# Two z slots of a fused two-block network moved ahead of the first round, by token tiles

## The chip, the cores and the metric

One core of one Trainium2 chip runs the whole program in one launch. The metric is the device time of one execution in microseconds (us), read as the median of the runs.

## The reference, cut to what matters

256 tokens of width 1024 pass through a first block of two layers and then a second block. The change lies at the start of the second block's mixer:

```python
h = rms_norm_2(x, g_mix[i])
proj = h @ w_in[i]
glu_a, glu_b, q, k, v, z, a_in, b_in, gate_a, gate_b = split_cols(proj, IN_SIZES)
...
qkv = silu(depthwise_conv(concat([q, k, v]), qkv_conv_w[i]))
g = -exp(a_log[i]) * softplus(a_in + dt_bias[i])      # a_in: 16 columns
beta = sigmoid(b_in)                                  # b_in: 16 columns
o_fwd = gated_delta_rule(q, k, v, g[:, :, 0], beta[:, :, 0])
...
o = rms_norm_2(o_fwd + o_bwd, delta_norm_g[i]) * silu(z)
```

x entering h is itself the output norm of the first block, so two norms follow one another there: the double norm (numbers 4 and 5 in the kernel). a_in and b_in together are the 32 columns called ab; z has 1024 columns.

## The kernel before, in words

**Weights.** All weights come as one stream of slots, in the order of stream_plan. A slot is 128 x 2048 float32 (1 MB): for a "pair", two tiles of 128 output columns over all eight tiles of the inner dimension; the slot of ab holds 32 columns only. SP's queue loads a slot into one of three raw buffers as soon as the slot three before is split. ACT rounds it to whi (split, L1784, or split_half, L1793) when TensorE is done with the slot three before. wlo = raw - whi is made by DVE (L2314), by POOL (L1075, in halves; for most slots of the rounds), or by both, POOL taking the first half (split_shared, L993) and DVE the second (L2310): the SHARED_SLOTS. Before, ab is DVE's, the slot ("qk", 0) is shared, and ("v", 0) is DVE's.

**Products.** The helper three (L1134 to L1136) makes hi x hi, hi x lo and lo x hi. A slot of the rounds takes 2 x 8 x 3 = 48 matrix multiplies, most of them feature-major: weights stationary, 256 tokens moving. A z slot is token-major: 128 tokens of the normalized input stationary, 256 weight columns moving; m of half_slot is then the token tile. ab is token-major too, before: 48 multiplies with 32 columns moving (ab_products).

**The double norm.** norm_behind_down(4, ...) on ACT and on DVE follows the down projection of the first block's last layer, whose last three slots are multiplied for token tile 0 first and then for tile 1. For each token tile: DVE adds the sums to x (L2442), multiplies by the gain (gain_x, L2425), scales (scale_x, L2433) and normalizes again (L2346); ACT takes the sums of squares (L1811, L1803); POOL the powers (L971, and L978 to L981). TensorE turns the tile to feature-major (turn_norm, L1158), ACT rounds it (L1866), DVE makes its low half (lows, L2416). Between these steps ACT and DVE split the coming slots, in a fixed order.

**TensorE's order.** turn_norm(5, 0), ab for tile 0, six spins (spin, L1141: a multiply of the identity that fills time, two records each), turn_norm(5, 1), two spins, ab for tile 1, then the rounds. Bank 3 of PSUM holds ab's sums.

**The rounds.** There are ten, of eight ticks each. A slot fills two ticks, two parts in each, and between the parts stand small multiplies of one of eight heads: prepare (turns, L1439 at tick 3; L1449 at tick 5; L1466 and L1470 at tick 6), the inverse by levels for the head of the round before (level_turn L1491 at tick 0, steps L1509 to L1531), and the chain of the head before that (L1574 to L1601). DVE works the 31 taps of a long convolution into each tick beside that (L2762, TAP_COUNT in each tick). Rounds 0 to 4 have four slots, rounds 5 to 9 have three but the last. Before, round 1 holds qk1, z0, glu2, glu3, and round 3 qk3, z2, glu5, z3.

**Round 0 around the change.** DVE copies ab from its bank and prepares it (decay_inputs, L2648 to L2654), then splits the slot of ("v", 0); ACT at tick 1 takes exp, ln and tanh (decay_logs, L2185 to L2189, with a table load before each), between two halves of a split; DVE makes the decays at tick 2; ACT evacuates qk0 at tick 2 (L2004), DVE adds its taps (L2699), ACT takes tanh (L2026), DVE gates (L2740), TensorE turns the result at tick 3 (L1439), and at tick 4 sums the decays (L1418 to L1423).

The wait of half_slot on a bank's earlier reader (slot_read) goes by the ordinal of a slot in MIX_SLOTS, two banks taking turns.

## Time and profile before

| | before |
|---|---|
| median of 3 runs | 1242.95 us (1240.95 to 1244.08) |
| span of the profiled execution | 1239.0 us |
| PE (matrix multiplies) busy | 1211.3 us, 98% |
| PE weight loads busy | 1109.0 us, 90% |
| DVE busy | 846.4 us, 68% |
| ACT busy | 703.4 us, 57% |
| POOL busy | 300.7 us, 24% |

The span runs from the first to the last instruction. The profile gives no other time for its own execution; the runs' median is 3.95 us above its span, which is what lies around the span. Positions below are us from the start of the span. Rows are of three kinds: the chain of work that ended last, the timeline (start, duration, engine, line, operation, output<-inputs, shapes, count, and in brackets the idle time before it with what ended it), and windows (busy time and number of instructions of each engine in a stretch, the granted clock of TensorE where 1.00 is full speed, the share of DMA time and GB/s).

### The profile page before, as it was taken

To read this page: it belongs to the slowest core of one execution; us is meant where nothing else is said; L and a number is where in the kernel's file an instruction comes from. 1 tells how busy PE (TensorE), PEld (TensorE's weight loads), DVE (VectorE), ACT (ScalarE), POOL (GpSimd) and SP (SyncE) were. 2 spreads that over 40 slices of the span, in tenths; PEclk is the share of its full clock that TensorE was granted. 3 is DMA by queue.
4 is the path that set the end of the run, shared out by engine and by line. 5 is a ranking of instruction groups with operands and counts; after the bars stand their busy time and mean duration, and the time that the engine had idled before them with its cause. 6 is when DMAs were issued, how large, how long until landed. Compare 5 with 4: busy or idle time off the path is not lost.

```text
span 1239.0 us, 21308 instructions
## 1 busy us (share of the span) xinstructions
PE 1211.3 (98%) x8590; PEld 1109.0 (90%) x8590; DVE 846.4 (68%) x1507; ACT 703.4 (57%) x1181; POOL 300.7 (24%) x251
## 2 busy tenths in 40 slices
PE   9999999999999999999999999999999999999997
PEld 7776899998877799998899999999988989999886
DVE  6796588874675678885558787788853555555457
ACT  5465576663467566664466666767665445444344
POOL 2170100000024000000166667565645210000000
PEclk9999999999999999999989999999998999999999
DMA  7633355555553355555333232232223555555542
GB/s 282 239 140 138 119 210 194 204 186 175 180 190 108 141 210 206 196 183 203 137 136 136 103 137 103 103 137 91 83 85 116 193 187 204 194 178 197 180 159 85
DMA packets 31586, 199.74 MB, mean 161 GB/s; under 512 B 4289, under 2 KB 6481, under 8 KB 8706
## 3 DMA queue, kind: packets, MB, share of 16 engines
q1 hardware_dynamic: 29506, 189.27, 42.3%
q0 software_dynamic: 1840, 8.60, 1.8%
q8 instruction: 68, 1.11, 0.4%
q10 hardware_dynamic: 144, 0.52, 0.1%
q14 instruction: 28, 0.23, 0.1%
HBM read 197.33 MB, written 1.05 MB: 160 GB/s over the span
## 4 chain that ended last, share of the span: by engine, by line
PE 85%; DVE 7%; ACT 4%; issue 2%; POOL 1%; DMA 0%; POOLq 0%; SPq 0%; ACTq 0%; DVEq 0%
PE ps L1134 25%; PE ps L1136 24%; PE ps L1135 24%; PE ps L1509 1%; PE ps L1525 1%; DVE ps L2762 1%; PE ps L1287 1%; PE ps L1306 1%; PE ps L1274 1%; PE ps L1158 1%; DVE conv L2699 1%; PE ps L1141 1%; PE ps L1227 1%; DVE wlo L2314 1%; ACT whi L1784 0%
## 5 line engine op out<-in xcount | busy, mean ns | idle before, releaser
L1134 PE MATMUL ps<-halves,whi 128*128 128x256 f32 x1472 | 415.7, 282 | 0.0
L1136 PE MATMUL ps<-halves,wlo 128*128 128x256 f32 x1472 | 410.2, 279 | 0.0
L1135 PE MATMUL ps<-halves,whi 128*128 128x256 f32 x1472 | 410.1, 279 | 0.0
L2314 DVE TENSOR_TENSOR wlo<-raw,whi 128x2048 fp32r<-128x2048 f32 (+1 forms) x139 | 315.2, 2270 | 126.0 <-ACT whi L1784 122.4
L1784 ACT ACTIVATE whi<-raw 128x2048 fp32r<-128x2048 f32 (+1 forms) x143 | 270.0, 1890 | 110.9 <-PE ps L1136 106.1
L1134 PEld LDWEIGHTS ps<-halves,whi 128*128 128x128 f32 x1472 | 278.2, 189 | 0.3 <-issue 0.2
L1135 PEld LDWEIGHTS ps<-halves,whi 128*128 128x128 f32 x1472 | 278.0, 189 | 0.1
L1136 PEld LDWEIGHTS ps<-halves,wlo 128*128 128x128 f32 x1472 | 277.9, 189 | 0.0
L1075 POOL TENSOR_TENSOR wlo<-raw,whi 128x1024 fp32r<-128x1024 f32 x72 | 173.9, 2425 | 53.5 <-ACT whi L1793 53.1
L1134 PE MATMUL ps<-whi,halves 128*128 128x512 f32 (+4 forms) x440 | 151.8, 345 | 3.8 <-DVE halves L2416 3.6
L971 POOL TENSOR_TENSOR rstd<-sumsq,half_power 128x1 f32<-128x1 f32 x14 | 11.1, 796 | 594.2 <-ACT xn L1811 422.4
L1136 PE MATMUL ps<-whi,halves 128*128 128x512 f32 (+4 forms) x440 | 147.4, 335 | 0.0
L1135 PE MATMUL ps<-wlo,halves 128*128 128x512 f32 (+4 forms) x440 | 147.1, 334 | 0.0
L1134 PE MATMUL ps<-whi,hhi 128*128 128x512 f32 x264 | 102.8, 390 | 0.5 <-DVE hf L2633 0.5
L1135 PE MATMUL ps<-wlo,hhi 128*128 128x512 f32 x264 | 102.7, 389 | 0.0
L1136 PE MATMUL ps<-whi,hlo 128*128 128x512 f32 x264 | 102.7, 389 | 0.0
L1134 PEld LDWEIGHTS ps<-whi,halves 128*128 128x128 f32 x440 | 83.2, 189 | 17.0 <-issue 8.8
L2762 DVE SCALAR_TENSOR_TENSOR ps<-glu_in,par,ps 128x256 f32<-128x256 f32 x224 | 94.8, 486 | 0.0
L1136 PEld LDWEIGHTS ps<-whi,halves 128*128 128x128 f32 x440 | 83.2, 189 | 9.0
L1135 PEld LDWEIGHTS ps<-wlo,halves 128*128 128x128 f32 x440 | 83.3, 189 | 7.5
L1962 ACT ACTIVATE cv<-ps,par 128x256 f32<-128x256 f32 x88 | 44.9, 561 | 76.8 <-PE ps L1136 70.5
L1793 ACT ACTIVATE whi<-raw 128x1024 fp32r<-128x1024 f32 x72 | 76.5, 1064 | 8.1 <-PE ps L1136 8.1
(333 smaller groups left out, 1821.5 us busy)
## 6 DMA issues: line engine op xcount, KB each, us to landing
raw<-in_stream SPq DMA_DIRECT2D x176, 1024.0 KB, 4.8
gain<-in_gains POOLq DMA_DIRECT2D x7, 512.0 KB, 6.1
bias<-in_rel POOLq DMA_DIRECT2D x1, 1536.0 KB, 9.0
raw<-in_stream SPq DMA_DIRECT2D x2, 648.0 KB, 7.3
cst<-in_consts POOLq DMA_DIRECT2D x1, 1280.5 KB, 5.9
raw<-in_stream SPq DMA_DIRECT2D x2, 528.0 KB, 4.1
x<-in_x SPq DMA_DIRECT2D x2, 512.0 KB, 4.4
out<-xn SPq DMA_DIRECT2D x4, 256.0 KB, 2.2
```

The lines of the kernel that those rows point to most:

```text
L1075: pool.tensor_tensor(wlo[:, n % RING, c], raw[:, n % RAW, c], whi[:, n % RING, c].bitcast(F32), ALU.subtract).then_inc(*S["pool_weights_lo ...
L1134: nc.tensor.matmul(out, a_hi, b_hi, start=start, stop=False)
L1135: nc.tensor.matmul(out, a_hi, b_lo, start=False, stop=False)
L1136: return nc.tensor.matmul(out, a_lo, b_hi, start=False, stop=stop)
L1141: nc.tensor.matmul(ps[:, bank, 0:P], ident, ident, start=True, stop=True)
L1158: last = nc.tensor.transpose(ps[:, 4 + 2 * t + half, i * P:(i + 1) * P], xn[:, t, (4 * half + i) * P:(4 * half + i + 1) * P], ident)
L1227: last = nc.tensor.transpose(ps[:, 3, i * P:(i + 1) * P], temp[:, b % 2, t, i * P:(i + 1) * P], ident)
L1784: act.activation(used(whi, n), used(raw, n), ACT.Copy).then_inc(*S["weights_high"].one((n, 1)))
L1793: act.activation(whi[:, n % RING, c], raw[:, n % RAW, c], ACT.Copy).then_inc(*S["weights_high"].one((n, half)))
L1962: act.activation(cv[:, j % 2, m, :], ps[:, up_bank(j), m * TOK:(m + 1) * TOK], ACT.Identity, bias=par_at(f"conv_b{li}", c), scale=par_at(f ...
L2314: dve.tensor_tensor(used(wlo, n), used(raw, n), used(whi, n).bitcast(F32), ALU.subtract)\
L2762: dve.scalar_tensor_tensor(odd_taps[:, :] if k == 29 else sums, src, w, sums, ALU.mult, ALU.add)\
```

## The change

Two of the four z slots, z0 and z1, leave rounds 1 and 2 (and z2 moves up from round 3 to round 2 into z1's place), so that rounds 1 and 3 have three slots where they had four. z0 and z1 stand ahead of ab in the stream and are multiplied as soon as a token tile of the double norm is there: both for tile 0, two spins, both for tile 1. Both are shared slots. ab comes after them and becomes feature-major: its 32 columns stationary, 256 tokens moving, 24 multiplies. DVE copies the 32 x 256 result to SBUF, TensorE turns it back in the first round behind the first part of qk0, and DVE takes it from there. ACT takes the second square of tile 0 ahead of a split. qk0 and v0 are split by DVE alone, each after the evacuation of a z slot by ACT (tanh) and DVE.

```diff
--- before.py
+++ after.py
@@ -85,6 +85,8 @@
         for j in range(FT):
             pair((f"up{layer}", j), ("ffn_w_up", layer), j * P, FF + j * P)
         down(f"down{layer}", ("ffn_w_down", layer), FT)
+    for key, weight, a, b in OPENING:
+        pair(key, (weight, 0), a, b)
     plan.append(("narrow", "ab", ("w_in_2", 0), 6144, 32))
     for round_ in ROUNDS:
         for key, weight, a, b in round_:
@@ -101,6 +103,11 @@
     return plan
 
 
+def z_slots():
+
+    return [(("z", j), "w_in_2", 5120 + 2 * j * P, 5120 + (2 * j + 1) * P) for j in range(KT // 2)]
+
+
 def rounds():
 
 
@@ -109,9 +116,9 @@
 
     glu = [(("glu", j), "w_in_2", j * P, 1024 + j * P) for j in range(KT)]
     gates = [(("gates", j), "w_in_2", 6176 + j * P, 7200 + j * P) for j in range(KT)]
-    z = [(("z", j), "w_in_2", 5120 + 2 * j * P, 5120 + (2 * j + 1) * P) for j in range(KT // 2)]
+    z = z_slots()
     out = [(("conv_out", i), "w_conv_out_2", 2 * i * P, (2 * i + 1) * P) for i in range(KT // 2)]
-    other = [glu[0:2], [z[0]] + glu[2:4], [glu[4], z[1]], [z[2], glu[5], z[3]], [glu[6], gates[0]],
+    other = [glu[0:2], glu[2:4], [glu[4], z[2]], [glu[5], z[3]], [glu[6], gates[0]],
              [glu[7]] + gates[1:2], gates[2:3], gates[3:5]]
     made = []
     for r in range(HEADS):
@@ -137,6 +144,7 @@
 JOINS_SECOND = {1: 1, 2: 2}
 PRODUCT_BANK = (3, 3, 3, 3, 6, 6)
 ROUNDS = rounds()
+OPENING = z_slots()[0:2]
 
 
 EVEN_BLOCKS = [("idx", 1536, 324), ("qb", 1860, 512), ("kb", 2372, 512), ("vb", 2884, 512),
@@ -353,6 +361,8 @@
     "early_turned": "and feature-major in its bank, (layer, j)",
 
     "gained": "x times the gain of norm 4 in xn, (t, half)",
+    "ab_copied": "decay's and beta's inputs, feature-major, copied from bank 3",
+    "ab_turned": "and token-major in bank 3",
     "ab_abs": "absolute value of the decay's input, all of ab read from its bank",
     "act_step": "exp of minus the absolute value; exp(a_log)",
     "ab_ln": "ln(1 + exp)",
@@ -526,12 +536,12 @@
                   ("proj", 3, 1): (2, 0), ("proj", 3, 2): (2, 1), ("proj", 5, 1): (4, 0), ("proj", 5, 2): (4, 1),
                   ("proj", 6, 1): (5, 0), ("proj", 6, 2): (5, 1)},
          "odd": {("proj", b + 1, 1 + t): (b, t) for b in range(4) for t in range(TT)}}
-SPINS = {0: (2, 3, 0), 1: (8, 2, 0), 2: (0, 0, 4), 3: (8, 2, 0), 5: (0, 0, 2), 6: (0, 4, 0), 7: (0, 0, 0)}
+SPINS = {0: (2, 3, 0), 1: (8, 2, 0), 2: (0, 0, 4), 3: (8, 2, 0), 5: (0, 0, 4), 6: (0, 4, 0), 7: (0, 0, 0)}
 SPIN_BANK = {1: 7, 3: 7}
 LEAD = RING
 EARLY = 2
 SPIN_BANK[5] = 2
-AB_SPINS = (6, 2)
+OPENING_SPINS = (2, 2)
 TURN_ORDER = {layer: list(turns.values()) for layer, turns in TURNS.items()}
 INDEX_AT = {("proj", 2, 1): (0, 1), ("proj", 2, 2): (2, 3), ("proj", 2, 3): (4, 5), ("proj", 3, 0): (6, 7)}
 FORGET_ROWS_AT = ("proj", 1, 3)
@@ -543,7 +553,7 @@
 
 
 
-MIX_SLOTS = [("ab", -1, 0)] + [(slot[0], r, 2 * i) for r, slots in enumerate(ROUNDS) for i, slot in enumerate(slots)] \
+MIX_SLOTS = [(slot[0], -1, 2 * i) for i, slot in enumerate(OPENING)] + [(slot[0], r, 2 * i) for r, slots in enumerate(ROUNDS) for i, slot in enumerate(slots)] \
     + [(("delta_out", i), len(ROUNDS), 0) for i in range(KT // 2)]
 ORDINAL = {key: n for n, (key, _, _) in enumerate(MIX_SLOTS)}
 READ_BY_ACT = {"gates"}
@@ -568,7 +578,7 @@
 
 def tanh_order():
 
-    order = []
+    order = [slot[0] for slot in OPENING]
     for r in range(len(ROUNDS)):
         for i in range(TICKS):
             key = finished_slot(r, i)
@@ -914,7 +924,7 @@
 
         POOL_SLOTS = [slot_of[key] + AHEAD for key, r, tick in MIX_SLOTS if 0 <= r < len(ROUNDS)]
 
-        SHARED_SLOTS = [slot_of[key] for key in (("up0", 1), ("up1", 1), ("qk", 0), ("up2", 1))]
+        SHARED_SLOTS = [slot_of[key] for key in (("up0", 1), ("up1", 1), ("z", 0), ("z", 1), ("up2", 1))]
 
         o_junk = ab[:, 3:5, :, :].rearrange("p a t c -> p (a t c)")
 
@@ -1037,7 +1047,8 @@
                 deviation(4, t)
                 deviation_5(t)
                 if t == 0:
-                    split_shared(("qk", 0))
+                    for key, *_ in OPENING:
+                        split_shared(key)
 
             pool.memset(sum_row[:, :].bitcast(F32), 0.0).then_inc(*S["rows_cleared"].one("mixer"))
             pool.memset(glu_in[:, :, :], 0.0).then_inc(*S["glu_cleared"].one())
@@ -1371,7 +1382,7 @@
                 n, o = slot_of[key], ORDINAL[key]
                 if m == 0 and part == 0:
                     wait_low(pe, n)
-                    if o >= 3:
+                    if o >= 2:
                         pe.wait_ge(*slot_read(MIX_SLOTS[o - 2][0]))
                 if key[0] == "z":
                     wh = used(whi, n).rearrange("p (k c) -> p k c", k=KT)
@@ -1393,19 +1404,32 @@
                 if m == 1 and part == 1:
                     last.then_inc(*S["weights_used"].one(n))
 
-            def ab_products(t):
+            def opening(t):
+
+                turn_norm(5, t)
+                for key, *_ in OPENING:
+                    for half in range(2):
+                        if key == OPENING[0][0]:
+                            wait_split(5, t, (half,))
+                        half_slot(key, t, half)
+
+            def ab_products():
 
                 n = slot_of["ab"]
-                if t == 0:
-                    wait_low(pe, n)
+                wait_low(pe, n)
                 wh, wl = used(whi, n), used(wlo, n)
                 for kt in range(KT):
-                    if kt % 4 == 0:
-                        wait_split(5, t, (kt // 4,))
-                    last = three(ps[:, 3, t * 32:(t + 1) * 32], xhi[:, kt, t * P:(t + 1) * P], xlo[:, kt, t * P:(t + 1) * P],
-                                 wh[:, kt, :], wl[:, kt, :], kt == 0, kt == KT - 1)
-                if t:
-                    last.then_inc(*S["weights_used"].one(n))
+                    last = three(ps[0:32, 3, 0:TOK], wh[:, kt, :], wl[:, kt, :], xhi[:, kt, :], xlo[:, kt, :],
+                                 kt == 0, kt == KT - 1)
+                last.then_inc(*S["weights_used"].one(n))
+
+            def turn_ab():
+
+                pe.wait_ge(*S["ab_copied"].at())
+                for t in range(TT):
+                    last = nc.tensor.transpose(ps[:, 3, TOK + t * 32:TOK + (t + 1) * 32], odd_taps[0:32, t * P:(t + 1) * P],
+                                               ident[0:32, 0:32])
+                last.then_inc(*S["ab_turned"].one())
 
             def decay_sums():
 
@@ -1710,11 +1734,10 @@
                 up(li, 2 * li + 1)
                 down(f"down{li}", FT, hhi, hlo, lambda kt: pe.wait_ge(*S["hidden_low"].at((li, kt))))
 
-            for t in range(TT):
-                turn_norm(5, t)
-                ab_products(t)
-                if t == 0:
-                    spin(*AB_SPINS)
+            opening(0)
+            spin(*OPENING_SPINS)
+            opening(1)
+            ab_products()
             for r in range(len(ROUNDS)):
                 for i in range(TICKS):
                     if r == 0 and i == 4:
@@ -1722,6 +1745,8 @@
                     level_first(r - 1, i)
                     if slot_at(r, i):
                         half_slot(slot_at(r, i), i % 2, 0)
+                    if r == 0 and i == 0:
+                        turn_ab()
                     chain_first(r - 2, i)
                     if i == 7:
                         query_products(r)
@@ -1839,9 +1864,9 @@
 
                 split(last)
                 square(k, 0)
-                split(last + 1)
                 if k == 4:
                     square(5, 0)
+                split(last + 1)
                 split(last + 2)
                 round_turned(5 if k == 4 else k, [(0, 0), (0, 1)])
                 square(k, 1)
@@ -2217,6 +2242,9 @@
                 up(li)
                 norm_behind_down(2 * li + 2, slot_of[(f"down{li}", FT // 2 - 1)])
 
+            for j, (key, *_) in enumerate(OPENING):
+                evacuate(key)
+                split(slot_of["ab"] + 1 + j)
             for r in range(len(ROUNDS)):
                 for i in range(TICKS):
                     if r == 0 and i == 1:
@@ -2641,11 +2669,16 @@
                 dve.tensor_tensor(plo[:, :, :], ps[:, up_bank(FT - 2), :].rearrange("p (k c) -> p k c", k=2),
                                   phi[:, :, :].bitcast(F32), ALU.subtract).then_inc(*S["p_low"].one())
 
+            def copy_ab():
+
+                dve.wait_ge(*S["weights_used"].at(slot_of["ab"]))
+                dve.tensor_copy(odd_taps[0:32, :], ps[0:32, 3, 0:TOK]).then_inc(*S["ab_copied"].one())
+
             def decay_inputs():
 
-                dve.wait_ge(*S["weights_used"].at(slot_of["ab"]))
+                dve.wait_ge(*S["ab_turned"].at())
                 dve.wait_ge(params2_loaded, 16)
-                link(dve.tensor_copy(ab[:, 0, :, :], ps[:, 3, 0:64].rearrange("p (t c) -> p t c", t=2)))
+                link(dve.tensor_copy(ab[:, 0, :, :], ps[:, 3, TOK:TOK + 64].rearrange("p (t c) -> p t c", t=2)))
                 dt = row_at["dt_bias_2"].unsqueeze(1).broadcast_to([P, TT, 16])
                 link(dve.tensor_tensor(ab[:, 0, :, 0:16], ab[:, 0, :, 0:16], dt, ALU.add))
                 link(dve.tensor_scalar(ab[:, 1, :, 0:16], ab[:, 0, :, 0:16], -1.0, None, ALU.mult))
@@ -2948,8 +2981,12 @@
                 up(li)
                 norm_behind_down(2 * li + 2, slot_of[(f"down{li}", FT // 2 - 1)])
 
+            for j, (key, *_) in enumerate(OPENING):
+                split(slot_of["ab"])
+                evacuate(key, 0)
+                split(slot_of["ab"] + 1 + j)
+            copy_ab()
             decay_inputs()
-            split(slot_of["ab"] + AHEAD)
             for r in range(len(ROUNDS)):
                 for i in range(TICKS):
                     if r == 0 and i == 2:
```

## Rows read from the trace of the kernel before

**Rows 1.** The page's chain of work that ended last, share of the span by engine.

```profile
PE 85%; DVE 7%; ACT 4%; issue 2%; POOL 1%; DMA 0%; POOLq 0%; SPq 0%; ACTq 0%; DVEq 0%
```

**Rows 2.** Timeline, PE, opening to round 0's first turn.

```profile
615.03 1.03 PE L1158 MATMUL ps<-ident,xn 128*128 128x128 f32 x8
...
617.27 0.25 PE L1134 MATMUL ps<-whi,halves 128*128 128x32 f32 x1 [1.20 <-DVE halves L2416]
...
620.42 2.91 PE L1141 MATMUL ps<-ident 128*128 128x128 f32 x12
...
628.59 0.36 PE L1134 MATMUL ps<-halves,whi 128*128 128x256 f32 x1
...
633.15 0.28 PE L1135 MATMUL ps<-halves,whi 128*128 128x256 f32 x1
...
635.98 0.28 PE L1135 MATMUL ps<-halves,whi 128*128 128x256 f32 x1
...
641.68 0.66 PE L1439 MATMUL ps<-ident,conv 128*128 128x128 f32 x4
```

**Rows 3.** Window in round 0: us, PE, PEld, DVE, ACT, POOL, clock, DMA, GB/s.

```profile
629.60:633.00 3.40, 3.40 (x19) 3.40 (x17) 2.42 (x4) 3.34 (x6) 2.95 (x1) 0.51 0.00 0
```

**Rows 4.** Windows by round (1, 3, 5, 6, 7), from one L1491 to the next.

```profile
660.74:695.06 34.32, 34.17 (x285) 33.58 (x286) 28.82 (x70) 22.61 (x48) 23.97 (x14) 1.00 0.35 124
...
732.29:768.21 35.92, 35.92 (x307) 35.59 (x306) 29.23 (x70) 24.16 (x55) 24.13 (x17) 1.00 0.33 118
...
805.61:837.30 31.69, 31.07 (x260) 30.19 (x258) 26.45 (x64) 21.24 (x52) 20.14 (x15) 1.00 0.37 134
837.30:871.50 34.20, 32.39 (x262) 31.14 (x263) 29.82 (x73) 23.15 (x56) 19.31 (x14) 1.00 0.27 93
871.50:904.10 32.60, 31.33 (x260) 30.25 (x258) 27.45 (x67) 21.54 (x53) 19.26 (x14) 1.00 0.27 98
```

**Rows 5.** Timeline, ACT, double norm and round 0.

```profile
612.57 1.93 ACT L1784 ACTIVATE whi<-raw 128x2048 fp32r<-128x2048 f32 x1 [1.24 <-PE ps L1136]
...
631.22 0.23 ACT L2185 ACTIVATE ab<-ab 128x32 f32<-128x32 f32 x1
...
634.41 0.23 ACT L2189 ACTIVATE ab<-ab 128x32 f32<-128x32 f32 x1
634.55 1.04 ACT L1793 ACTIVATE whi<-raw 128x1024 fp32r<-128x1024 f32 x1
636.07 0.84 ACT L2004 ACTIVATE conv<-ps,par 128x256 f32<-128x256 f32 x2 [0.47 <-PE ps L1136]
```

**Rows 6.** Timeline, DVE, the same stretch.

```profile
617.63 1.29 DVE L2425 TENSOR_TENSOR xn<-x,gain 128x512 f32<-128x512 f32 x2
...
619.95 1.22 DVE L2310 TENSOR_TENSOR wlo<-raw,whi 128x1024 fp32r<-128x1024 f32 x1
...
628.78 0.23 DVE L2648 COPY ab<-ps 128x64 f32<-128x64 f32 x1 [2.39 <-PE ps L1136]
...
629.74 2.29 DVE L2314 TENSOR_TENSOR wlo<-raw,whi 128x2048 fp32r<-128x2048 f32 x1
```

**Rows 7.** Timeline, POOL, the same stretch.

```profile
614.57 2.36 POOL L993 TENSOR_TENSOR wlo<-raw,whi 128x1024 fp32r<-128x1024 f32 x1 [2.16 <-ACT whi L1784]
617.87 0.86 POOL L971 TENSOR_TENSOR rstd<-sumsq,half_power 128x1 f32<-128x1 f32 x1 [0.94 <-ACT junk L1811]
...
630.05 4.22 POOL L1075 TENSOR_TENSOR wlo<-raw,whi 128x1024 fp32r<-128x1024 f32 x1 [6.88 <-ACT whi L1793]
```

**Rows 8.** Timeline, POOL's and then DVE's half of an earlier shared slot.

```profile
135.94 2.40 POOL L993 TENSOR_TENSOR wlo<-raw,whi 128x1024 fp32r<-128x1024 f32 x1 [43.54 <-ACT whi L1784]
...
137.80 1.62 DVE L2310 TENSOR_TENSOR wlo<-raw,whi 128x1024 fp32r<-128x1024 f32 x1
```

**Rows 9.** Timeline, ACT: a table load ahead of a wait.

```profile
358.28 1.28 ACT L1937 ACT_TABLE_LOAD   x1
362.25 0.40 ACT L1937 ACTIVATE prob<-prob,lowest 128x128 f32<-128x128 f32 x1 [2.69 <-DVE lowest L2579]
```

## The prediction

> **What bounds the kernel now.** I read the chain of waits first: 85% of it is TensorE, 7% DVE, 4% ACT [rows 1]. So a change pays by taking time out of TensorE's order, and costs by making TensorE wait. Then the timeline of TensorE around the change [rows 2]: the down projection ends at 615.03, the turn of tile 0 and a wait of 1.20 us lead to ab at 617.27, spins fill from 620.42, round 0 begins at 628.59, and the first turn of round 0 (L1439) comes at 641.68. These 26.65 us are one half of the question. The other half is rounds 1 and 3, which lose a slot each. The windows by round show what a slot is worth there [rows 4]: round 3 with four slots took 35.92 us, round 7, also without a v slot, 32.60 with three, round 5 31.69.
>
> **What is removed.** Multiplies with 256 moving columns follow one another every (635.98 - 633.15)/24 = 0.118 us at full clock [rows 2], so a slot of 48 is 5.65 us. Two slots leave rounds 1 and 3 on balance: at most 11.3 us. But a product also hides DVE, which stays: the taps per tick don't change, since the tick in which the next glu slot is ready moves only earlier and the counts per tick are used up before and after. Only the evacuations of two z slots, about 0.7 us each on DVE (a 512-wide pass of the same kind is half of a 1.29 us pair [rows 6]), leave the rounds. DVE was busy 26.45, 29.82 and 27.45 us in the three-slot rounds 5, 6 and 7, and these lasted 5.2, 4.4 and 5.2 us more than that [rows 4]: DVE and its waits set their length. Round 3 keeps 29.23 - 0.7 = 28.5 us of DVE, plus 4.7 is 33.2: it gives back 2.7. Round 1 keeps 28.1 us, has no chain yet (fewer dependent steps), and TensorE's own 34.3 - 5.65 = 28.7; I put it halfway between 28.7 and 28.1 + 5 = 33.1, at 31: 3.3 back. Together 6.0 us, bounds 4.4 (both at DVE plus 5) and 11.3.
>
> **The opening, step by step.** Nothing moves up to 615.03. The turn of tile 0 and the wait for its low half stay: 617.3.
>
> - *z0's low half.* Today one shared slot, ("qk", 0), is split by POOL at 614.57 in 2.36 us and by DVE at 619.95 in 1.22 [rows 6, 7]. ACT could round that slot at 612.57 [rows 5]. Now ACT rounds z0 about 611.0 to 612.9 (the second square goes first) and z1 to 614.8. POOL can start z0 at 613.0, but DVE normalizes from two SBUF inputs until 613.6 and then wants its own half of z0. That the two engines keep each other out is in the rows: POOL's 2.4 us split took 4.22 beginning 0.3 us after a DVE split of 2.29 [rows 6, 7], and DVE's 1.22 us half took 1.62 when it met the end of POOL's [rows 8]. With DVE first, POOL has z0 from 614.9 to 617.3, and TensorE starts z0 at 617.45, as now within 0.2 us.
> - *z1's low half.* POOL goes on with z1, 617.3 to 619.7. DVE's gain_x for tile 1, at 617.63 today [rows 6], now meets it and waits to 619.7. POOL's power for tile 1, at 617.87 today [rows 7], comes behind z1 too, at 619.7 or later. gain_x takes 1.29, scaling 0.9, then DVE's half of z1 1.22: ready at about 623.2 where the half that stands there today was ready at 621.17. TensorE ends z0 of tile 0 at 617.45 + 2.83 = 620.3 and stands still until 623.3: 3.0 us. What is queued behind this wait is all of TensorE.
> - *The rest.* z1 of tile 0 2.83; two spins 0.45; turn of tile 1 0.9; four spins 0.9, which nearly cover ACT's and DVE's rounding, 0.2 more; z0 and z1 of tile 1 5.65; ab, 24 multiplies. The trace has none with 32 stationary columns and 256 moving; the bounds are 0.118 as the other 256-wide ones and the low clock's 0.21, and nothing gives a gain over 0.118; taken 0.118, 2.83. Round 0 then begins at 623.3 + 13.75 = 637.05.
> - *Clock.* Where the granted clock was 0.51, TensorE started 19 multiplies in 3.40 us where 0.118 would give 29 [rows 3]: a loss of about 1.3 us each such stretch. Today it fell after the wait at 617.27 and the 32-column multiplies. The new wait of 3 us may bring it down while z1 is multiplied; half a stretch taken, 0.7. Bounds none and two stretches, 2.6.
>
> Round 0 at 637.75, that is 9.15 us later than 628.59.
>
> **Round 0 to its first turn.** Call X the end of z1 for tile 1; TensorE has ab done at X+2.8 and the first part of qk0 at X+4.25.
>
> - *The copy of ab.* ACT evacuates z1 and rounds v0 until X+2.7; DVE has qk0 (2.29), z1's evacuation (0.7), then v0 (2.29) [rows 6] until X+5.2, and only then copies ab, 0.45. TensorE turns it at X+5.8 instead of X+4.25: a wait of 1.55, and 0.3 for the two turns. Behind this wait stands the whole of qk0's second part. The bounds of the copy and the turns, which no row shows: 0.2 (the 64-wide copy took 0.23 [rows 6]) to 0.7, and 0.2 to 0.7.
> - *The logs.* DVE prepares ab until X+7.1. ACT has exp to tanh from 631.22 to 634.64, 3.4 us [rows 5]; the load of exp's table ahead of it is hidden in the wait, as the load at 358.28, which ran at once while its ACTIVATE waited 2.69 us more [rows 9]. The same hides the extra load of tanh's table for z0, while ACT waits for z0's products. So ACT is free at X+10.6, then has half a split, 1.04 [rows 5].
> - *qk0.* Its products end at X+10.3; ACT evacuates it at X+11.65 instead of X+10.4. From there to the turn it took 641.68 - 636.07 = 5.6 us [rows 2, 5]: X+17.25. TensorE is there at X+16.05. A wait of 1.2 where today it is 0.2.
> - *Given back.* The low clock in round 0 today, 1.3 [rows 3].
>
> Sum for this part: 1.55 + 0.3 + 1.0 - 1.3 = +1.55 us. Later steps of round 0 have room: DVE has few taps yet, and the late half of glu0 is low at about X+14, while TensorE needs it at X+20.
>
> **The sum.** +9.15 + 1.55 - 6.0 = +4.7 us on the profiled span, 1239.0 to 1243.7; with the 3.95 us between span and median, 1247.6. I give 1247.5.
>
> **A rule weighed.** The Trainium skill, SBUF — State Buffer, "Who interferes with whom", says that a DVE instruction with two SBUF inputs contends with a GpSimd instruction that reads SBUF, and that whichever issues first keeps the shared pair for its whole instruction while the other stands fully blocked. The trace agrees at both places named above, the 4.22 and the 1.62 us. By a rule of shared bandwidth the two halves of z1 would stretch a little and TensorE's wait would be about 1 us, the sum +2; by this rule it speaks against the change.
>
> **The rivals.**
>
> - *Matrix work is all that counts.* Count only TensorE's own time: the opening 18.7 us long instead of 13.56, +5.1; turns +0.3; clock -1.3; the wait at L1439 -0.2; two slots -11.3: -7.4, 1235.5. For it: 85% of the chain. Against it: the three-slot rounds, which TensorE alone would have ended at 35.92 - 5.65 = 30.3 and which took 31.69 and 32.60 [rows 4]. It decides from where the waits (3.0 for z1, 1.55 for the copy, 1.2 for qk0, 5.3 not given back by the rounds, 0.7 clock, some 0.4 small) come to less than 7.4; to be faster by over 0.3% (3.7 us, about what a measurement of this kernel can tell from no change) they must be under 3.7.
> - *No collision at z1.* POOL and DVE fall so that z1 is ready at 621.2, as the half in its place now [rows 6]: 2.1 less wait and no fall of the clock, 0.7: +1.9, 1244.8. For it: DVE's adds and lows read PSUM and leave POOL room until 617.6. Against it: POOL has 4.8 us of splits from 613.0 on, which end at 617.8 at best.
> - *POOL first.* POOL gets z0 at 613.6, DVE's half waits to 616.0, and the add of tile 1 and the lows of tile 0 stand behind it. TensorE starts z0 at 619.4, after 3.5 us of standing, z1 at about 624.4; the clock falls for at least a stretch. 1.1 + 1.3 more, with a second stretch 3.7: +7 to +8.5, 1250 to 1252. For it: POOL asks for z0 before DVE does. Against: the order at 613.6 is a toss.
> - *The change does nothing it says.* z's multiplies by tiles are as many as before and cost the same, so no work is saved but ab's 24 multiplies; that is in the sum already.
>
> **How the numbers follow.** Chances: forecast 45%, no collision 22%, POOL first or more low clock 18%, matrix work 15%. The forecast's own range is 1244.5 to 1250.5 by the bounds of the clock and the rounds. Slower by over 0.3%, above 1246.7: 29 of the forecast's 45, all 18, 1 of the second, 48%. Faster, below 1239.2: 11 of the last 15 and 2 of the second, 13%. Within: 39%. Range 1240 to 1253, which leaves about 10% below and 8% above.
>
> **What would show it.** Right: in the opening, TensorE idle 2 to 4 us between z0 and z1 of tile 0 with DVE's L2310 as the releaser, and L2425 of tile 1 starting after 619; a wait of 1 to 2 us before the turns of ab, with the copy behind v0's split; L1439 near 652 (+10.7); rounds 1 and 3 near 31 and 33 us. Wrong: z1's first multiply before 621.5; rounds 1 and 3 both under 30.5 us, which would make the kernel faster by more than it loses in the opening; or a fall of the clock of more than two stretches.

## The result: slower by 0.58%

The changed kernel took 1248.88 us (median of 19 runs) beside 1241.9 us for the kernel before, a ratio of 1.0058 with a 95% interval of 1.004 to 1.0077: by the ratio 7.2 us slower (5.0 to 9.6). The lowest, the median and the highest of the 19 runs lie 8.5, 7.0 and 9.7 us above those of the kernel before. The profiled execution took 1249.72 us and has a span of 1247.9. The page of the changed kernel, its span, its busy times and its chain by engine:

```profile
span 1247.9 us, 21256 instructions
...
PE 1210.4 (97%) x8564; PEld 1106.0 (89%) x8564; DVE 854.1 (68%) x1510; ACT 702.5 (56%) x1179; POOL 293.6 (24%) x248
...
PE 82%; DVE 9%; ACT 5%; issue 3%; POOL 1%; DMA 0%; POOLq 0%; DVEq 0%; ACTq 0%
```

TensorE has 26 multiplies fewer and is busy 0.9 us less; the chain has moved to DVE and ACT (from 11% to 14%, [rows 1]). Not all of the 8.9 us between the two spans are the change's. The turn of tile 0 stands at 619.64 instead of 615.03 [rows 2], and TensorE's order ahead of it is the same. The last section comes back to that. From that turn to the last L1491, that of round 8 (L1515 in the changed kernel; rounds 1 to 8 have one each, and the rounds shown in [rows 4] run from one to the next), it is 299.49 us instead of 289.05: +10.4. TensorE's timeline there, to be laid beside [rows 2]:

```profile
619.64 0.60 PE L1169 MATMUL ps<-ident,xn 128*128 128x128 f32 x4
620.50 0.66 PE L1169 MATMUL ps<-ident,xn 128*128 128x128 f32 x4 [0.27 <-DVE xn L2374]
625.58 0.58 PE L1145 MATMUL ps<-whi,halves 128*128 128x256 f32 x1 [4.42 <-DVE halves L2444]
...
644.07 0.28 PE L1145 MATMUL ps<-halves,whi 128*128 128x256 f32 x1
...
646.57 0.31 PE L1430 MATMUL ps<-ident,odd_taps 32*128 32x32 f32 x2 [0.93 <-DVE odd_taps L2675]
...
658.82 0.66 PE L1463 MATMUL ps<-ident,conv 128*128 128x128 f32 x4 [1.84 <-DVE conv L2773]
```

The first z product comes 5.94 us after the turn, where ab's first came after 2.24. Round 0 begins at 644.07, 24.43 us after the turn (13.56 before). Then there are the two waits that were forecast, for ab's copy (0.93) and for qk0's gated result (1.84). The windows (columns as in [rows 3]) of the two z slots of tile 0, of the stretch behind L1463, and of rounds 1 and 3 [rows 4]:

```profile
625.58:633.05 7.47, 7.47 (x48) 7.47 (x49) 5.28 (x8) 2.00 (x5) 3.90 (x6) 0.73 0.59 231
...
658.82:663.50 4.68, 4.68 (x29) 3.77 (x29) 2.08 (x6) 3.48 (x14) 4.27 (x5) 0.67 0.42 144
```

```profile
680.95:712.07 31.12, 29.27 (x238) 28.04 (x238) 26.86 (x65) 19.83 (x45) 19.95 (x12) 1.00 0.38 136
...
749.36:783.15 33.79, 32.19 (x260) 31.49 (x259) 28.17 (x68) 21.56 (x52) 20.37 (x16) 0.95 0.35 125
```

Rounds 1 and 3 gave back 3.20 and 2.13 us. In round 3 the granted clock was 0.95 in this execution; in the profiles below where it was 1.00, round 3 took 33.3 or 33.4 us, which is 2.5 or 2.6 back. Why the opening is so late stands in the timelines of DVE (first fence) and POOL (second):

```profile
616.83 3.62 DVE L2374 SCALAR_TENSOR_TENSOR xn<-x,rstd,gts 128x512 f32<-128x512 f32 x2 [1.09 <-POOL rstd L991]
620.37 3.36 DVE L2338 TENSOR_TENSOR wlo<-raw,whi 128x1024 fp32r<-128x1024 f32 x1
623.66 1.28 DVE L2470 SCALAR_TENSOR_TENSOR x<-ps,x 128x512 f32<-128x512 f32 x2
...
646.11 0.41 DVE L2675 COPY odd_taps<-ps 32x256 f32<-32x256 f32 x1
...
647.18 1.31 DVE L2683 TENSOR_TENSOR ab<-ab,rows 128x32 f32<-128x32 f32 x1
```

```profile
617.50 5.16 POOL L1003 TENSOR_TENSOR wlo<-raw,whi 128x1024 fp32r<-128x1024 f32 x2 [0.81 <-ACT whi L1809]
...
645.53 2.90 POOL L1086 TENSOR_TENSOR wlo<-raw,whi 128x1024 fp32r<-128x1024 f32 x1 [13.95 <-ACT whi L1818]
```

POOL took its half of z0 at 617.50, between DVE's two instructions of the normalization (its half of z0 and that of z1 are one line here, 5.16 us for both). The second of them waited (the pair took 3.62 us instead of about 1.42), then DVE's own half of z0 waited for POOL's half of z1 (3.36 instead of 1.22 [rows 6]). Tile 1's adds and tile 0's low halves, behind these on DVE, began at 623.66 and 624.86, and TensorE stood until 625.58.

### The profile page after: what moved, and what is told of

Read it like the earlier page. It is cut to its first block, busy times and chain, and to the rows that moved or that the text cites. A ratio compares the mean times of both kernels' runs of the same rounds, so it can differ in the third digit from the quotient of the medians.

```text
span 1247.9 us, 21256 instructions
## 1 busy us (share of the span) xinstructions
PE 1210.4 (97%) x8564; PEld 1106.0 (89%) x8564; DVE 854.1 (68%) x1510; ACT 702.5 (56%) x1179; POOL 293.6 (24%) x248
## 4 chain that ended last, share of the span: by engine, by line
PE 82%; DVE 9%; ACT 5%; issue 3%; POOL 1%; DMA 0%; POOLq 0%; DVEq 0%; ACTq 0%
PE ps L1145 24%; PE ps L1147 23%; PE ps L1146 23%; PE ps L1533 1%; DVE ps L2795 1%; PE ps L1549 1%; DVE conv L2732 1%; PE ps L1298 1%; PE ps L1317 1%; PE ps L1285 1%; DVE wlo L2342 1%; PE ps L1169 1%; ACT whi L1809 1%; PE ps L1152 1%; PE ps L1238 1%
## 5 line engine op out<-in xcount | busy, mean ns | idle before, releaser
L1809 ACT ACTIVATE whi<-raw 128x2048 fp32r<-128x2048 f32 x145 | 273.5, 1889 | 108.6 <-PE ps L1147 104.0
L1086 POOL TENSOR_TENSOR wlo<-raw,whi 128x1024 fp32r<-128x1024 f32 x68 | 163.1, 2407 | 63.1 <-ACT whi L1818 62.7
L1145 PE MATMUL ps<-whi,halves 128*128 128x512 f32 (+3 forms) x424 | 148.6, 351 | 7.0 <-DVE halves L2444 6.9
L1147 PE MATMUL ps<-whi,halves 128*128 128x512 f32 (+3 forms) x424 | 144.0, 340 | 0.0
L1146 PE MATMUL ps<-wlo,halves 128*128 128x512 f32 (+3 forms) x424 | 143.8, 339 | 0.0
L1145 PEld LDWEIGHTS ps<-whi,halves 128*128 128x128 f32 x424 | 80.9, 191 | 20.1 <-issue 6.9
L1147 PEld LDWEIGHTS ps<-whi,halves 128*128 128x128 f32 x424 | 80.9, 191 | 9.0
L1818 ACT ACTIVATE whi<-raw 128x1024 fp32r<-128x1024 f32 x68 | 72.2, 1063 | 5.3 <-PE ps L1147 5.3
```

The costliest lines, as they stand in the source:

```text
L1086: pool.tensor_tensor(wlo[:, n % RING, c], raw[:, n % RAW, c], whi[:, n % RING, c].bitcast(F32), ALU.subtract).then_inc(*S["pool_weights_lo ...
L1145: nc.tensor.matmul(out, a_hi, b_hi, start=start, stop=False)
L1146: nc.tensor.matmul(out, a_hi, b_lo, start=False, stop=False)
L1147: return nc.tensor.matmul(out, a_lo, b_hi, start=False, stop=stop)
L1809: act.activation(used(whi, n), used(raw, n), ACT.Copy).then_inc(*S["weights_high"].one((n, 1)))
L1818: act.activation(whi[:, n % RING, c], raw[:, n % RAW, c], ACT.Copy).then_inc(*S["weights_high"].one((n, half)))
```

## The experiments

All edits are of the changed kernel unless said, and the diffs shown are condensed. Line numbers shift by a few from kernel to kernel (L1462 of e1 is L1463 of the changed kernel); the table goes by the changed kernel's. The table gives each ratio to the kernel before, and from each profile, in us after the turn of tile 0: the first z product, the turn L1463 of round 0 (26.65 before), the first L1515 of round 1 (45.7 before), and the length of rounds 1 and 3.

```
kernel            ratio, 95% interval       z0     L1463  L1515  round 1  round 3
changed           1.0058 (1.0040-1.0077)    5.94   39.18  61.31   31.12    33.79
changed, again    one run                   5.95   38.78  60.92   31.3     33.4
e1_z0_dve         1.0055 (1.0033-1.0078)    2.65   35.57  54.62   31.3     33.3
e1, again         one run                   2.65   35.29  55.77   31.1     33.3
e2_no_pool        1.0050 (1.0028-1.0071)    2.65   37.88  60.06   31.3     33.3
e3_copy_first     1.0137 (1.0098-1.0176)    5.94   39.49  63.26   31.1     33.3
e4_thin_taps      one run                   5.94   39.08  61.22   29.96    32.44
e10_thin_both     one run                   5.94   39.89  60.5    29.96    32.44
e5_logs_late      1.0077 (1.0048-1.0106)    2.65   37.29  60.96   31.3     33.9
e6_ab_by_tiles    1.0042 (1.0016-1.0069)    2.65   35.91  54.96   31.1     33.3
e7_spins          1.0101 (1.0052-1.0150)    5.96   38.63  60.80   31.2     33.3
e8_best           1.0100 (1.0046-1.0154)    2.66   37.40  60.51   30.95    32.91
e9_one_z          0.9995 (0.9973-1.0016)    2.66   29.64  51.80   31.25    35.91
```

**POOL out of z0's split, and out of both.**

```diff
-SHARED_SLOTS = [... ("z", 0), ("z", 1), ...]     # e1: only ("z", 1); e2: neither
-for key, *_ in OPENING: split_shared(key)        # POOL; e1: split_shared(("z", 1)); e2: gone
```

> The changed kernel, but DVE alone makes z0's low half (2.3 us) and only z1 is shared with POOL. Lock theory: POOL's two splits back to back (617.50 to 622.66 in the changed kernel) held up DVE's second half of the normalization by 2.2 us and its half of z0 by 2.1 us, and with these tile 1's adds and tile 0's lows. Now POOL can't start before z1 is rounded, so the first z product begins 2.2 to 3.2 us after the turn of tile 0 instead of 5.94, with a wait of about 1 us before z1 of tile 0; from the turn to round 0's turn L1463 about 34 to 36 us instead of 39.2. Time near 1245, 3 to 4 us below the changed kernel. Rival (the first z product is late by ACT's order, or by the moved square, not by POOL): the start stays 5 us or more after the turn, and the time is unchanged at about 1249.

> The changed kernel, with POOL taking no part of z0 or z1: DVE splits both whole. DVE gets 2.4 us more work than with both shared. Lock theory: even so the first z product starts about 2.2 to 3.2 us after the turn of tile 0, and z1 of tile 0 waits about 2 us for DVE's whole split; turn to L1463 about 35 to 37 us instead of 39.2; time 1245 to 1247. Rival (the engines share the port's bandwidth, POOL's help is worth its 2.4 us): slower than the changed kernel by 1 to 2 us, 1250 or more.

TensorE of e1, and then DVE and POOL:

```profile
618.92 1.03 PE L1168 MATMUL ps<-ident,xn 128*128 128x128 f32 x8
621.57 0.39 PE L1144 MATMUL ps<-whi,halves 128*128 128x256 f32 x1 [1.62 <-DVE halves L2443]
...
625.99 0.39 PE L1144 MATMUL ps<-whi,halves 128*128 128x256 f32 x1 [1.32 <-DVE wlo L2337]
```

```profile
616.11 1.42 DVE L2373 SCALAR_TENSOR_TENSOR xn<-x,rstd,gts 128x512 f32<-128x512 f32 x2 [1.09 <-POOL rstd L991]
617.44 2.28 DVE L2341 TENSOR_TENSOR wlo<-raw,whi 128x2048 fp32r<-128x2048 f32 x1
...
618.58 3.37 POOL L1003 TENSOR_TENSOR wlo<-raw,whi 128x1024 fp32r<-128x1024 f32 x1 [2.61 <-ACT whi L1808]
```

With DVE doing more of the work, the first product comes 3.3 us sooner, in both kernels; the normalization is back at 1.42. Now POOL is the one that waits (3.37 instead of 2.4, until DVE's whole split is over). ACT's order and the moved square are as in the changed kernel, so it was POOL's early half, and the port that it and DVE keep from each other. e2 pays 2.12 us before z1 of tile 0, as expected; its L1463, at 37.88, lies above the 35 to 37 expected. The gain in whole time is smaller than the profile's 7 us for e1 and 1.5 for e2: the ratios' intervals overlap that of the changed kernel, and the ratios alone don't show a gain. So the port's part in the opening is shown in the profiles, and its share of the 7.2 us is not.

**The changed kernel and e1 a second time.**

> The changed kernel once more, for a second look. Theory (POOL has the port first by the order of the code, not by chance): the first z product again 5.9 us after the turn of tile 0, the wait before L1463 again 1.8 us. What may differ is the clock behind it, and the pace of the 256-wide products in the three up projections, 113.5 or 118 ns each.

> The kernel of e1_z0_dve once more. Its profile showed no low clock at all, while every other kernel with a wait of 1.8 us before L1463 but that one had 3 us lost behind it. Theory (chance of the phase): the waits are the same, 1.6, 1.3, 1.15 and 1.86 us, and low clock appears in some stretch this time; turn to L1515 of round 1 56 to 58 us instead of 54.6. Rival (e1's shorter first wait keeps the clock up): again none.

The waits come again to 0.1 us, but for z1's in e1, 0.96 instead of 1.32, and the copy's in the changed kernel, 1.15 instead of 0.93. So POOL's precedence belongs to the code. The clock does not: e1's first profile has none of it low between 612 and 680 us, its second has a stretch behind L1462, where the window 650.25:656.00 shows 0.76.

**The copy of ab ahead of v0's split.**

```diff
-                split(slot_of["ab"] + 1 + j)
-            copy_ab()
+                if j: copy_ab()
+                split(slot_of["ab"] + 1 + j)
```

> The changed kernel, with DVE's copy of ab ahead of its split of v0 instead of behind it. Theory: the wait of 0.93 us before the turns of ab goes, and ab's chain (DVE, then exp, ln, tanh on ACT) is about 2 us earlier, so the wait of 1.84 us before L1463 falls to under 0.5 and the low clock behind it (660.7 to 665, some 3 us lost by round 1's L1515) may not come. L1463 2 to 2.5 us earlier, the time 2 to 5 us below the changed kernel, 1244 to 1247. Rival (L1463 waits for qk0's own chain, taps and tanh on DVE and ACT, not for the logs): the wait before ab's turns goes but the one before L1463 grows by as much; nothing gained.

The wait before ab's turns is gone, but L1463 waits longer:

```profile
646.19 2.15 DVE L2683 TENSOR_TENSOR ab<-ab,rows 128x32 f32<-128x32 f32 x1
...
644.67 3.61 POOL L1086 TENSOR_TENSOR wlo<-raw,whi 128x1024 fp32r<-128x1024 f32 x1 [13.55 <-ACT whi L1818]
...
658.68 1.06 PE L1463 MATMUL ps<-ident,conv 128*128 128x128 f32 x4 [3.57 <-DVE conv L2773]
```

(The lines are of DVE, POOL and TensorE.) v0's split now stands between the copy and the rest of ab's work, and the add of dt_bias, a 32-wide instruction of 0.19 us where it is alone, takes 2.15: POOL has begun a split, itself held up until DVE's ended. In the changed kernel the same add took 1.31. The rival's result came, by the port and not by qk0's own chain. Its four runs give a ratio of 1.0137, 0.8% above the changed kernel's, while from the turn to the last L1515 its profile has only 1.5 us more. Behind that it has 5.2 us more, with the third up stage at the slower of the two paces of the last section (427 products in 1070:1120, 444 in the changed kernel). Whether the other three runs have the same cause stays open.

**The logs behind qk0.** On e1:

```diff
-if r == 0 and i == 1: decay_logs()           # ACT, now at i == 2 behind evacuate
-if r == 0 and i == 2: decays()               # DVE, now at i == 3
```

> On top of e1_z0_dve: ACT takes exp, ln and tanh of ab after its evacuation of qk0 (tick 2) instead of before it, and DVE the decays at tick 3. Theory: what holds up the turn L1463 is ab's chain standing ahead of qk0 on ACT (in e1, conv L2028 began at 648.90, right behind the logs, 2 us after qk0's products). With the logs behind it the wait of 1.86 us before L1463 goes; the decays may now be late instead at L1442, by under 1 us. Turn of tile 0 to round 1's L1515: 52.5 to 54 us instead of 54.6. Time 1 to 2 us under e1. Rival (DVE is what is late, with the splits and the copy): L1463 stays at 35.5 us after the turn.

Neither the theory nor the rival: L1462 waits 3.94 us and comes 37.29 us after the turn. DVE (the first two lines), POOL and TensorE:

```profile
644.72 2.31 DVE L2683 TENSOR_SCALAR ab<-ab 128x32 f32<-128x32 f32 x1
...
654.71 2.35 DVE L2772 SCALAR_TENSOR_TENSOR conv<-tanh,conv 128x512 f32<-128x512 f32 x1 [1.14 <-ACT tanh L2050]
...
654.16 5.11 POOL L1085 TENSOR_TENSOR wlo<-raw,whi 128x1024 fp32r<-128x1024 f32 x2 [7.17 <-ACT whi L1817]
...
657.12 1.12 PE L1462 MATMUL ps<-ident,conv 128*128 128x128 f32 x4 [3.94 <-DVE conv L2772]
```

The later logs bunch POOL's halves together, and DVE's gating of qk0 from two SBUF inputs, 0.69 us alone (e1, changed), takes 2.35 behind POOL's split. The first line is a TENSOR_SCALAR with one SBUF input, 0.18 us alone (e1, changed), and it took 2.31 behind a split of POOL too. L1515 comes at 60.96, and 4.6 us of that are a stretch of low clock behind L1462: 23.67 us from there to L1514, at 0.79, where e1 took 19.05 at 1.00. So this edit alone doesn't tell what the logs' place is worth.

**ab by token tiles.** On e1, with ab multiplied token-major behind the z slots, no copy, no turns back:

```diff
-last = three(ps[0:32, 3, 0:TOK], wh[:, kt, :], wl[:, kt, :], xhi[:, kt, :], xlo[:, kt, :], ...)
+for t in range(TT): ... three(ps[:, 3, t * 32:(t + 1) * 32], xhi[..t..], xlo[..t..], wh[:, kt, :], wl[:, kt, :], ...)
```

> On top of e1_z0_dve: ab is multiplied by token tiles as before the change (48 multiplies with 32 columns moving, both tiles behind the z slots), so that the copy, the turns back and their wait are gone. Theory: the feature-major form saves 2.6 us of TensorE and gives back 1.15 (wait for the copy) and 0.24 (turns); but L1463 waits for ab's chain in any case, so the time of L1463 moves by less than 1 us and the whole is within 1 us of e1. Rival (TensorE's own time counts): 1.2 to 2.6 us slower than e1.

As the theory had it: L1515 54.96 us after the turn against 54.62 and 55.77, and no wait at L1463, though TensorE comes later. At the end of its 32-column multiplies (636.92 to 642.3) and behind them the clock is low, about 23 to 26 us after the turn (0.57 in 642.00:646.00). The feature-major form of ab, a part of the change, is worth nothing that these profiles show.

**Spins in the hole.**

```diff
-5: (0, 0, 4)
+5: (0, 18, 4)
```

> The changed kernel with 18 spins behind the turn of tile 0 (4 us of multiplies of the identity at full clock) where it stands still for 4.42 us. Theory (idle TensorE is what brings the clock down): no low clock in the first 15 us after the turn, the z slots of tile 0 take 5.7 us instead of 7.47; the first z product still 5.9 to 6.1 us after the turn, since DVE and POOL set that; turn to L1463 37 to 38 us instead of 39.2. The low clock after L1463 stays. Rival (the clock falls by its own, whatever TensorE does): the z slots of tile 0 again take over 7 us.

The windows of e7, of the hole with its spins and of tile 0's z slots:

```profile
624.15:630.11 5.96, 5.28 (x45) 4.84 (x43) 5.96 (x6) 1.81 (x3) 3.03 (x2) 1.00 0.12 22
630.11:638.00 7.89, 6.85 (x58) 6.65 (x59) 5.27 (x8) 1.99 (x5) 3.89 (x6) 1.00 0.62 238
```

The clock stays at 1.00 (2.4 GHz) where it was 0.73 (partly at 1.2 GHz), and the z slots take 5.9 us and a new wait of 1.04 for z1's low half. So it was the idle stretch that had brought the clock down. The Trainium skill, TensorE: Matmul & The Clock Gate, "What's actually happening", has the same cause, activity that releases the throttle; the trace agrees. Of the 1.6 us, 0.5 arrive at L1463. In the ratio of its four runs, 1.0101 (1.0052 to 1.0150), no gain shows.

**What holds a three-slot round.**

```diff
+if tick // TICKS in (1, 3) and k != 29: sums, src = sums[:, 0:16], src[:, 0:16]   # e4, e10
+if r in (1, 3): c = slice(half * SLOT // 2, half * SLOT // 2 + 16)                # e10, POOL's low halves
```

> The changed kernel with most long-convolution taps of rounds 1 and 3 cut to 16 of 256 columns: this leaves out part of the convolution, to take about 12 us of DVE's time out of each of the two rounds. Theory (DVE sets the length of a three-slot round): round 1 falls from 31.1 to about 28.7 us and round 3 from 33.8 to about 30.3, what TensorE alone would need, so that the two slots give back their 11.3 us. Rival (a three-slot round is held by the level steps' own chain of dependences, or by ACT and POOL): the rounds stay above 30.5 and 33. The opening is unchanged.

> As e4_thin_taps (taps of rounds 1 and 3 mostly cut to 16 columns), and POOL's low halves of the slots split in these two rounds cut to 16 columns as well: this leaves out parts of the convolution and of the weights' low halves. Theory (the port that DVE and POOL keep from each other holds the rest of a three-slot round): round 1 28.7 to 29.3 us and round 3 30.3 to 31, against 30.0 and 32.4 with thin taps alone. Rival (the dependent steps of a head's inverse hold it): within 0.3 us of 30.0 and 32.4.

Windows of rounds 1 and 3, e4 and then e10:

```profile
676.10:706.06 29.96, 28.89 (x239) 28.09 (x238) 19.96 (x67) 19.80 (x45) 19.94 (x12) 1.00 0.40 141
...
743.33:775.77 32.44, 30.89 (x260) 30.05 (x258) 20.55 (x68) 21.33 (x52) 20.07 (x15) 1.00 0.38 131
```

```profile
679.86:709.82 29.96, 28.88 (x238) 28.08 (x238) 19.97 (x67) 19.81 (x45) 6.83 (x12) 1.00 0.38 141
...
747.10:779.54 32.44, 30.88 (x259) 30.05 (x258) 20.56 (x68) 21.34 (x52) 7.14 (x15) 1.00 0.37 131
```

Taking 7 us from DVE in each round shortens round 1 by 1.2 us, and round 3 by 1.35, of which 0.4 or 0.5 are the low clock that the changed kernel's profile has there (33.3 or 33.4 at 1.00); taking another 13 from POOL, by nothing. DVE's load accounts for about half of what round 1 lacks to 28.7 and 0.3 of what round 3 lacks to 30.3. The rest is neither engine's load; ACT's was not varied. The dependent steps of a head are argued and not shown.

**The edits together, and three taps moved.** On e5:

```diff
+TAP_ROUND[1] = TAP_ROUND[3] = [8, 6, 0, 5, 3, 4, 4, 2]
+TAP_ROUND[2] = TAP_ROUND[4] = [8, 6, 0, 6, 2, 3, 7, 4]
```

> On top of e5_logs_late: three taps each of rounds 1 and 3 are moved to rounds 2 and 4, which have four slots. Theory (a part of a three-slot round is DVE's): rounds 1 and 3 lose 0.5 to 1 us each against 31.3 and 33.3, rounds 2 and 4 stay at 37.3 and 37.4 (DVE has 5 us of room there). In all 1 to 2 us under e5, about 1 us around the kernel before. Rival (only the chain of dependent steps holds these rounds): rounds 1 and 3 unchanged, rounds 2 and 4 longer.

Rounds 1 and 3 are 0.4 and 1.0 us shorter than in e5 (0.4 beside the 33.3 of the profiles with full clock there), rounds 2 and 4 are 1.0 and 0.8 longer (38.27 and 38.23). The room of DVE in a four-slot round was not room: nothing is won.

**One z slot.** Only z0 in the opening, split by DVE, with ten spins behind it; z1, z2 and z3 in rounds 2 and 3:

```diff
-OPENING = z_slots()[0:2]
+OPENING = z_slots()[0:1]
```

> Only z0 stands ahead of ab, split whole by DVE; z1, z2 and z3 stay in rounds 2 and 3, ab is feature-major, ten spins behind z0 of tile 0. Theory (one slot fits the hole that tile 1's chain leaves, the second doesn't; a slot gives back 2 to 3 us of its 5.65 in the rounds): round 0 begins 16 to 17.5 us after the turn of tile 0 (13.56 before), round 1 takes 31.1, round 3 its 35.9; the time is 0 to 2 us under the kernel before. Rival (any z slot there is a loss): 2 us or more over it.

```profile
641.70 0.38 PE L1142 MATMUL ps<-halves,whi 128*128 128x256 f32 x1 [0.56 <-DVE wlo L2338]
...
649.19 0.66 PE L1460 MATMUL ps<-ident,conv 128*128 128x128 f32 x4 [1.78 <-DVE conv L2769]
```

Window from L1460 to L1512, the changed kernel's L1463 to L1515:

```profile
649.19:671.35 22.16, 22.16 (x154) 20.82 (x154) 12.16 (x32) 12.60 (x33) 12.84 (x10) 0.85 0.34 118
```

The first line is a short wait for a low half of DVE's in round 0. The ratio is 0.9995 (0.9973 to 1.0016): no change that can be measured, the best of all forms tried, and not a version that beats the kernel before. In its profile round 0 begins 15.4 us after the turn (16 to 17.5 were expected), L1515 comes 6.1 us later than before and round 1 gives back 3.07, so the profile alone would say 3 us slower; the runs don't. The profiled execution is the slowest of the twelve, 1243.92 us with a mean granted clock of 0.993, and ten of the twelve have 0.997 or 0.998. The window shows where it lost: 22.16 us at 0.85, where the kernel before took 19.06 at 1.00. Without these 3.1 us the profile comes out even, as the runs do. That the other ten lack this very stretch is likely, and not shown. The ten spins are an edit of their own, which no run separates from the one slot less.

## Why the prediction was right, and where it was not

The time forecast was 1247.5, the measured 1248.88; the sum had +4.7 us over the kernel before, the runs +7.2, the profile +10.4 from the turn on. The direction and the reason were right: the waits of the opening and what the rounds don't give back outweigh the two slots. That the time is off by 1.4 us only is in part luck, since the kernel before had 1242.95 in its three runs then and 1241.9 in the nineteen beside the change. Windows from L1439, L1463 or L1462 to the next round's L1491, L1515 or L1514, of the kernel before, the changed one and e1:

```profile
641.68:660.74 19.06, 19.06 (x154) 18.25 (x154) 12.16 (x32) 12.63 (x33) 12.90 (x10) 1.00 0.35 123
...
658.82:680.95 22.13, 22.13 (x153) 20.78 (x153) 12.15 (x32) 12.60 (x33) 12.86 (x10) 0.85 0.31 117
...
654.49:673.54 19.05, 19.05 (x154) 18.25 (x154) 12.16 (x32) 12.61 (x33) 12.90 (x10) 1.00 0.36 138
```

By its steps:

- **The rounds' return**, 6.0 us forecast: 3.20 + 2.13 = 5.3 measured, 5.7 or 5.8 with full clock in round 3. That DVE is all of the reason was too simple: e4 and e10 leave half of it or more to something else. The lower bound had a slip: with DVE plus 5 in both rounds, 28.1 + 5 and 28.5 + 5 us, they give back 1.2 + 2.4 = 3.6, not 4.4.
- **z0's low half**, "with DVE first, POOL has z0 from 614.9". This is the step that failed, and the rival "POOL first" took its place. POOL asked when the prediction said it could (617.50 less the 4.61 of the later turn is 612.9, forecast 613.0); wrong was that DVE would hold it off until both instructions of the normalization were over. POOL got in between the two, even earlier than that rival had it, so z0 began 5.94 us after the turn and not 2.4 (or 4.4, by the rival). That cost 3.5 us more. Nor was the order a toss: all six profiles with POOL in z0's split have z0 at 5.94 to 5.96.
- **z1's low half**, a wait of 3.0: none, since z0 was as late as z1. With the 3.5 above, the port's price in the opening was sized nearly right and put in the wrong place. Where POOL was moved out of the way, the wait at z1 was there (1.32 and 0.96 in e1, 2.12 in e2).
- **Clock in the opening**, 0.7: 7.47 - 5.65 = 1.8, undone by the spins of e7. The size of a stretch was read a little low: the 19 multiplies of [rows 3] count three that began before the window, 16 began in it, so the 3.4 us lost 1.5 and not 1.3.
- So round 0 began 10.87 us late and not 9.15.
- **The copy's wait**, 1.55: 0.93. **The logs and qk0's wait**, 1.2: 1.84. The add of dt_bias behind POOL's split, 1.1 us, was not in the sum. The load of exp's table hid in the wait as forecast (645.41 to 646.69, its ACTIVATE at 648.96); the extra load for z0's tanh doesn't exist, ACT's timeline has none between 454.93 and 645.41. Round 0's start to L1463: +1.66, forecast +1.55.
- **Clock behind L1463**: not forecast. From L1463 to round 1's L1515 it took 22.13 us instead of 19.06; e12 and e11 have such a stretch too, e1 none. In all three windows above TensorE is busy throughout, and only the changed kernel's has a clock under 1.00: the 3.07 us are the clock's. Which of the waits before it brings it down isn't shown.
- The rule weighed, of a port that one engine keeps for its whole instruction, is what decided: three kernels show DVE instructions stretched by up to 2.2 us, of sizes from 32 to 1024 columns, and a small one ends when POOL's split does: at 648.49 and POOL's at 648.43 in the changed kernel, 648.34 and 648.28 in e3, 647.03 and 646.99 in e5.
- **Span and median.** The 3.95 us added to the span are not what lies around it. The profiled execution took 1249.72 us with a span of 1247.9, so that is 1.8, and the rest is the difference between executions. The forecast doesn't hang on it: 1242.95 + 4.7 is the same 1247.6. Nor does the forecast's own range follow from its bounds: 1244.5 to 1250.5 is narrower than the clock's and the rounds' bounds allow (rounds of 11.3 back alone make it 1242.2).

10.87 + 1.66 + 3.07 - 5.33 = +10.3 of the +10.4. The runs' +7.2 lies under it; the clock's stretches and the paces below differ from one execution to the next. (The profiled execution has a mean clock of 0.990; fifteen of the nineteen have 0.991 to 0.994.) Of the prediction's own signs, the idle time between z0 and z1 of tile 0 isn't there, and one of those for being wrong is: low clock cost 1.8 us in the opening and 3.07 behind L1463, more than two stretches of 1.5.

## What to carry to other kernels

Work moved into a hole of the critical engine brings its helpers with it: here two slots of multiplies were to fill it, but their splits stood on the very DVE that was to end the hole. Before giving POOL a long instruction, list which of DVE's instructions on the path read SBUF while it runs, however short: those with two SBUF inputs above all, but in e5 a TENSOR_SCALAR with one took 2.31 us instead of 0.18. And a slot taken from a stage gives back its own time only as far as nothing else holds the stage: 5.3 of 11.3 us here.

## What was not expected of the hardware

The 256-column products of an up projection run at one of two paces, 50 us holding 444 or 427 of them, with the granted clock at 1.00 in both and no wait. Windows of the kernel before (two stages) and of the changed one (the same two):

```profile
200.00:250.00 50.00, 50.00 (x444) 50.00 (x443) 41.93 (x64) 32.02 (x49) 0.00 (x0) 1.00 0.53 191
...
1060.00:1110.00 50.00, 50.00 (x427) 50.00 (x426) 27.22 (x27) 21.84 (x27) 0.00 (x0) 1.00 0.52 182
```

```profile
200.00:250.00 50.00, 50.00 (x427) 50.00 (x426) 40.73 (x63) 30.78 (x45) 0.00 (x0) 1.00 0.51 184
...
1070.00:1120.00 50.00, 50.00 (x444) 50.00 (x443) 27.87 (x29) 23.50 (x28) 0.00 (x0) 1.00 0.54 195
```

It is 113.5 against 118 ns each, some 4.4 us over a stage of about 1000. Each of the three up stages has its own pace in each execution: the changed kernel's first profile had the first of them slow and its second profile had all three fast, e1's first had the second slow and its second none, e8 had all three slow. Of the kernel before there is one profile, so whether the change shifts how often a stage is slow isn't known, and that could be a part of the ratios. In the changed kernel's profile the first up stage's pace is the 4.6 us ahead of the turn, and the last one's is -4.3 us later on; two such stages outweigh the effect measured. The up stages aren't alone in it: in the changed kernel's opening the z products of tile 0 follow one another every 0.113 us from 629.87 on, those of tile 1 every 0.118 from 635.73. What sets the pace isn't shown here. One profile beside another is to be compared by stages, and whole times only over many runs.
